# One comparison instead of four for the one-hots of the second half-index

## The reference

```python
i1 = jnp.take_along_axis(top_i[:, :, 0], best_c // PEER_TOPK, axis=-1)
i2 = jnp.take_along_axis(top_i[:, :, 1], best_c % PEER_TOPK, axis=-1)
experts = i1 * PEER_KEYS + i2
gate = jax.nn.softmax(best_s, axis=-1)
pre = jnp.einsum('td,thkd->thk', xt, expert_u[experts])
act = jax.nn.gelu(pre, approximate=False)
return jnp.einsum('thk,thkd->td', gate * act, expert_v[experts])
```

## Time and profile before

| | |
|---|---|
| median of three runs | 2309.12 us |
| the profiled execution | 2308.13 us |
| its span (first to last instruction) | 2306.3 us |
| outside the span | 1.83 us |
| PE busy, share of the span | 2050.8 us, 89% |
| DVE busy | 1583.5 us, 69% |
| POOL busy | 1159.3 us, 50% |
| ACT busy | 771.7 us, 33% |
| first to last comparison of the gates stage | 1266.5 to 1558.9 us |

### The profile page before, as it was taken

How to read it: one execution, slowest core, us unless ns; L and a number is a source line. 1 busy time by engine, 2 the same in 40 slices (tenths; PEclk the granted TensorE clock), 3 DMA queues, 4 the chain that set the end, 5 groups by cost and what they waited for, 6 DMA issues and landing times.

```text
span 2306.3 us, 34698 instructions
## 1 busy us (share of the span) xinstructions
PE 2050.8 (89%) x12706; PEld 1908.5 (83%) x12706; DVE 1583.5 (69%) x3094; ACT 771.7 (33%) x1228; POOL 1159.3 (50%) x632
## 2 busy tenths in 40 slices
PE   5999878786768897999998888889989999999998
PEld 5989744575748896998888887889979999999998
DVE  2478443344433202779986999994469999999996
ACT  3223133323221323444444334333323333333332
POOL 2336000031113232477676343437788888888884
PEclk9999787988958898999999999999989999999999
DMA  5664354243523254477778567769979998999894
GB/s 183 214 224 158 133 160 160 66 164 156 190 76 122 85 230 166 145 243 225 233 236 272 214 237 263 257 239 367 364 273 315 320 318 309 309 319 313 313 325 139
DMA packets 176598, 520.95 MB, mean 226 GB/s; under 512 B 15153, under 2 KB 86065, under 8 KB 170705
## 3 DMA queue, kind: packets, MB, share of 16 engines
q1 hardware_dynamic: 136560, 290.94, 36.7%
q0 software_dynamic: 36864, 134.23, 17.5%
q10 hardware_dynamic: 3056, 94.24, 10.7%
HBM read 456.81 MB, written 128.49 MB: 254 GB/s over the span
## 4 chain that ended last, share of the span: by engine, by line
DVE 42%; PE 40%; issue 6%; POOL 4%; DMA 4%; ACT 4%; SPq 0%; ACTq 0%; DVEq 0%; PEldq 0%; POOLq 0%
DVE acc_g L1883 10%; DVE act_l L1867 9%; PE bank L2241 6%; PE bank L2242 6%; PE bank L2243 6%; DVE one L1561 6%; DVE one L1560 5%; DVE rows_g L1731 3%; POOL u_lo L1706 3%; PE twin L2241 2%; PE twin L2243 2%; PE twin L2242 2%; PE twin L492 1%; PE bank L511 1%; DMA w_raw<-wpq 1%
## 5 line engine op out<-in xcount | busy, mean ns | idle before, releaser
L1706 POOL TENSOR_TENSOR u_lo<-u_raw,u_hi 128x1024 fp32r<-128x1024 f32 x128 | 316.4, 2472 | 330.4 <-ACT u_hi L1686 329.8
L2241 PE MATMUL bank<-hn_hi,u_hi 128*128 128x416 f32 x1024 | 374.6, 366 | 33.4 <-POOL u_lo L1706 32.5
L1911 POOL TENSOR_TENSOR v_lo<-v_raw,v_hi 128x1024 fp32r<-128x1024 f32 x128 | 336.6, 2631 | 70.4 <-ACT v_hi L1836 69.2
L2242 PE MATMUL bank<-hn_lo,u_hi 128*128 128x416 f32 x1024 | 363.6, 355 | 0.0
L2243 PE MATMUL bank<-hn_hi,u_lo 128*128 128x416 f32 x1024 | 362.1, 354 | 0.0
L1883 DVE SCALAR_TENSOR_TENSOR acc_g<-rows_g,coef,acc_g 128x1024 f32<-128x1024 f32 x127 | 289.9, 2282 | 17.1 <-DMA rows_g<-ev,idx_g 16.6
L2242 PE MATMUL bank<-a_lo,v_hi 128*128 128x416 f32 x768 | 269.1, 350 | 0.0
L2241 PE MATMUL bank<-a_hi,v_hi 128*128 128x416 f32 x768 | 269.1, 350 | 0.0
L2243 PE MATMUL bank<-a_hi,v_lo 128*128 128x416 f32 x768 | 269.0, 350 | 0.0
L2241 PEld LDWEIGHTS bank<-hn_hi,u_hi 128*128 128x128 f32 x1024 | 196.0, 191 | 49.1 <-POOL u_lo L1706 46.3
L1867 DVE TENSOR_TENSOR act_l<-act_l,gin 128x416 f32<-128x416 f32 x128 | 229.2, 1791 | 0.6 <-DMA act_l<-acts_dram 0.5
(11 more groups left out here) (414 smaller groups left out, 4629.3 us busy)
## 6 DMA issues: line engine op xcount, KB each, us to landing
u_raw<-eu SPq DMA_DIRECT2D x128, 512.0 KB, 4.9
v_raw<-ev SPq DMA_DIRECT2D x128, 512.0 KB, 4.7
k_s<-kc ACTq DMA_DIRECT2D x29, 1104.0 KB
v_s<-vc ACTq DMA_DIRECT2D x29, 1104.0 KB
acts_dram<-act_c SPq DMA_DIRECT2D x128, 208.0 KB, 3.9
gates_dram<-gst ACTq DMA_DIRECT2D x8, 3328.0 KB, 12.3
gin<-gates_dram SPq DMA_DIRECT2D x32, 832.0 KB, 8.1
act_l<-acts_dram SPq DMA_DIRECT2D x64, 416.0 KB, 5.6
```

Source lines behind the costliest of these rows:

```text
L1706: nc.gpsimd.tensor_tensor(out=u_lo[s][:], in0=u_raw[2 * (x % 2) + s][:], in1=u_hi[s][:].bitcast(F32), op=ALU.subtract).then_inc(dn["ulo"], 1)
L1911: nc.gpsimd.tensor_tensor(out=v_lo[f % 4][:], in0=v_raw[f % 4][:], in1=v_hi[f % 4][:].bitcast(F32), op=ALU.subtract).then_inc(dn["vlo"], 1)
L2241: nc.tensor.matmul(out, ah, bh, start=first and i == 0, stop=False)
L2242: nc.tensor.matmul(out, ah, bl, start=False, stop=False)
```

## The change

The four comparisons that made `one2` of a group, one for each token, become one `tensor_tensor` comparison over 128 x 512: the row 0 to 127 repeated four times, against four columns of `picks_t`, each repeated 128 times. `asc_p` is still read from PSUM and `picks_t` from SBUF. It stands ahead of the four comparisons for `one1`, which stay. Buffers, waits and the order on the other engines are the same.

```diff
             for n in range(GBLOCKS * QUADS):
                 dve.wait_ge(ff["gate_mm"], n + 1)
+                tt(out=one2[n % HOT][:], in0=bc(asc_p, 1, 4), in1=bc(picks_t[:, 1, 4 * n:4 * n + 4], 2, PK), op=ALU.is_equal)
                 for j in range(4):
                     c = 4 * n + j
-                    ts(one2[n % HOT][:, j, :], asc_p, picks_t[:, 1, c:c + 1], None, ALU.is_equal)
                     last = ts(one1[n % HOT][:, j, :], asc_p, picks_t[:, 0, c:c + 1], picks_t[:, 2, c:c + 1], ALU.is_equal, ALU.mult)
                 last.then_inc(ff["ones"], 1)
                 if n % QUADS % 2 and n >= HOT:
                     dots(dve, NT, 1)
```

## The result

Four runs of the kernel after gave a median of 2272.96 us (2263.65 to 2278.58), four of the kernel before 2306.93 us. The ratio is 0.9845, with a 95% interval of 0.9811 to 0.9878: the kernel after is faster, by 1.2 to 1.9%. The profiled execution of after took 2271.49 us, its span is 2269.7 us. The forecast was 2271 us, in a range of 2260 to 2289.

The account below looks back on a forecast made before the run. DVE's list was taken to bound the gates stage; it falls 46 us to 247, plus some 8 for waits gives about 255, saving 38. Profiled 2308.1 - 38 = 2270 us, median 2271; range 2260 to 2289.

Parts of the forecast that it names:

- The bound: Gates stage: it ends when DVE's list, 293.3 of 293.8 us, is done; PE is next, busy 254.47 us.
- The added comparison: DVE, per group: one 128 x 512 two-tensor comparison costs 0.60 us from start to start, 0.72 as the bound.
- only three instruction starts are dropped: DVE, new comparison: 512 elements are streamed as before, so nothing goes below 0.60 us.
- The Trainium skill's estimate: DVE, PSUM operations at 120 cycles plus one per element: 0.375 us saved per group, 39 us of list.
- two bounds: PE in the gates stage: 241 us by its steps in time order, 254.5 us by recorded busy time.
- some 8 for waits: Gates stage: waits added to DVE's 247 us list, giving a stage of about 255 us.
- short waits on both sides: Gates stage: DVE and PE, with nearly equal lists, run side by side, stage about 255 us.
- The dots' rows: Gates stage: shortest lead shrinks from 10.66 to 9.3 us, twice the landing; one stall of about 5 us possible.
- The clock: PE in the gates stage: granted 1.00 (2.4 GHz) from 1300 to 1550 us, with no reason to be granted less.
- take half: Rival, gates stage: about half of PE's 38.0 us of waits stay, gain about 20 us, 2289 us; chance 0.13.
- given back behind the stage: Rival, behind the gates stage: DMA sets the last dot's end, time stays at about 2308 us; chance 0.06.
- POOL did not block: Rival, new comparisons: POOL blocking costs each 0.60 us, 62 against 46 saved, 16 us slower, 2325; chance 0.04.

Follow-up runs that it names:

- both last edits: Kernel after with the gates stage's eight blocks written out on PE, ACT and SP, and row fetches three dots ahead instead of two: median 2257.32 us.
- the second execution of after: Kernel after once more, unchanged, on the same chip as the written-out kernel with fetches three ahead: median 2268.70 us.

## Why the prediction was right, and where its reasons were not

- *The bound.* That DVE's list set the stage before held, and so did the forecast that PE's would be nearly as long behind the change. The removed 0.44 us per group gave 45.8 us of list, and the kernel with both last edits shows the list bare: forecast 247 us, stage 247.2, DVE busy for all of it.
- *The added comparison.* Forecast 0.60 us from start to start, with 0.72 as the other bound; measured 0.60. The four `one1` comparisons were left at 0.32 each; measured 1.27 to 1.28 for the four.
- *Why it is cheaper: this reason was wrong in part.* The prediction said that "only three instruction starts are dropped". Of the 0.44 us per group, 0.24 went with the exchange of the instruction (1.04 to 0.80) and 0.20 with the merging (0.80 to 0.60). The sum came out right because both ends of the difference, 0.26 and 0.60, were read from rows; the story between them was not tested by any row. That a value per partition may cost something could have been seen: 0.26 and 0.32 us stood in the earlier trace rows for comparisons with one and two of them.
- *The Trainium skill's estimate*, from VectorE: DVE Perf Modes, the section on the TRN2 errata, gave 39 us for DVE's list. Its one fixed term for all operations from PSUM has no part for the fetched value, and its large comparison, 658 ns, lies between the 600 ns from start to start and the recorded 679. The list fell by 46; that the stage fell by 39 as well is a coincidence, due to waits which that estimate does not have.
- *PE.* Its list was put at 241 to 254 us by two bounds. In the run with both last edits PE was busy for 239.9 of the 247.2 us, and stood 7.9 before the one-hot matmuls until DVE was done: the lower bound is the right one. Taking 255 us for the stage, from DVE's 247 and some 8 for waits, came within 1.4 us of the 253.6 measured, where DVE was idle for some 6; the second execution of after had 251.4. The 8 for waits came from no row, so a part of that closeness is luck.
- *Which waits: sized right, placed in part.* The "short waits on both sides" were expected between the two engines. DVE waited for PE for 0.7 us only; 5.1 us were waits for rows. PE waited 9.2 us for DVE and 4.2 for its own instructions.
- *The dots' rows: mis-sized.* The shortest lead of a dot in the stage was to shrink from 10.66 to 9.3 us, with a single stall of about 5 possible. It shrank to 5.8 us (fetched at 1413.12, used at 1418.92), although that dot did not wait; the median landing grew from 4.6 to 6.4 us with a DMA share of 0.75 instead of 0.68, and there were three stalls of 5.1 us in all. The single stall came much as it was priced: 4.0 us, behind a landing of 14.7.
- *The clock.* "A PE that idles less gives no reason to be granted less" missed the 2.9 us in which PE stood at the turn of its loop: the granted clock from 1400 to 1404 us was 0.59, so for most of them it was the lower of the two levels, 1.2 and 2.4 GHz. This does not follow each time: in the second profile of after PE stood 2.6 us at the same place, and the clock behind it (1404 to 1408) was 1.00.
- *The rivals.* PE did not take half: its waits for the last comparison fell from 38.0 us over 37 times to 9.2 over 10. Nothing was given back behind the stage beyond 1.7 us. POOL did not block: all 104 comparisons took 669 to 692 ns. That this rests on where the inputs lie, and not on which of them comes second, is shown by the run with both in SBUF. It agrees with the rule of the Trainium skill, SBUF — State Buffer, section Who interferes with whom, that a DVE instruction with two SBUF inputs contends with a GpSimd instruction that reads SBUF.

## What to carry to other kernels

A train of small instructions is priced by the distance between starts, and the difference of two such distances is safer than any account of why they differ. Before a saving on one engine is written down, make the list of the next engine for the same stage: here 46 us of DVE's list went and 39 came, and of the missing 7 some 6 went to two small kinds of waits of DVE (5.1 for rows, 0.9 before the new comparisons) that did not show while it was late all the time. When merging operations on VectorE beside a busy GpSimd, keep one input in PSUM: the same merge with both in SBUF gave 11 us instead of 39.

## What the runs showed of the hardware that was not expected

- A comparison over 128 elements with a PSUM input holds DVE for 0.20 to 0.21 us without a value per partition (as a two-tensor operation, or against a constant), for 0.26 with one, and for 0.31 to 0.32 with two and a multiplication. Four two-tensor comparisons and four against a constant gave the same stage, 267.5 us.
- At the turn of the loop over the blocks PE stood without a releaser: in after for 1.3 us and, some 3 us later, for 2.9. The longer of the two was 2.4 to 3.4 us in nine profiles with the loop; in that of the kernel before the two were 0.9 and 0.6 us, and why so little is open. Behind the 2.9 us in after the first matmuls took 0.55 to 0.72 us instead of 0.35 to 0.46; behind the 2.6 us in its second profile they did not. Written out, the stalls were gone.
- Blocking between POOL and DVE goes both ways: with both inputs in SBUF, `u_lo` rose from 2389 to 2679 ns on average as the comparisons rose from 679 to 946.
